# Norms between layers of a four-layer kernel: the last tile's squares go from ScalarE straight to TensorE, two norms share a root, and weights are asked for ahead of a wait

## The chip, the cores and the metric

The kernel runs on one core of one Trainium2 chip. The metric is the time of one execution on the device, in microseconds (us); lower is better. The times below are medians of several executions.

## The reference

The kernel computes four residual layers on 512 tokens of width 1024, all in fp32. What matters here is what stands between the layers: each begins with an RMS norm of the residual x, and the first block ends with a norm whose output feeds the next norm.

```python
def rms_norm(x, g):
    xf = x.astype(jnp.float32)
    y = xf * lax.rsqrt(jnp.mean(xf * xf, axis=-1, keepdims=True) + EPS)
    return (y * g.astype(jnp.float32)).astype(x.dtype)

# first block: an even layer (convolution and RWKV), then an odd one (attention over selected keys)
for l in range(2):
    h = rms_norm(x, norm_g[l]) * (1.0 + scale[:, None, :]) + shift[:, None, :]
    ...
    x = x + gate[:, None, :] * out
x = rms_norm(x, final_g)
# second block: a linear recurrence (lru), then attention with a forget gate (fox)
h = rms_norm_2(x, norm_g_2[0]); x = x + lru_mixer(h, ...)
h = rms_norm_2(x, norm_g_2[1]); x = x + fox_mixer(h, ...)
return rms_norm_2(x, final_g_2)
```

## The kernel before

x lies transposed, as 8 tiles of 128 channels by 512 tokens. Every projection is done at fp32 precision by three matmuls: the weight w and the input h are each split into a rounded part (`w_hi`, `h_hi`) and the rest (`w_lo`, `h_lo`). A weight block of 128 columns comes by DMA into one of four `raw` buffers (SyncE's queue, `weights_in`, L429), ScalarE rounds it in two halves (`round_half`, L463), GpSimd makes the rest in two halves (`rest_half`, L481), and TensorE multiplies (`project`, L498 to L500; the fox values `project_values`, L539 to L541). A raw buffer may be overwritten once GpSimd has made the rest of the block four places earlier; a split buffer (two of them, NSPLIT) is free once TensorE has projected the block two places earlier.

The program of each engine is written out by hand: `merge` interleaves streams of steps by due times that stand in the code, and all waits are on semaphores. So each engine runs a fixed list in order, and a wait holds back all that stands behind it on that engine. SyncE's list of transfers is such a list too (`sync_program`, L3005 on).

Each layer ends with an output projection in 16 half blocks (cb, part), cb being one of 8 tiles of x: `out_tensor`, `out_scalar`, `out_vector`. When a tile's second part is projected, VectorE adds it to x (L991, L993). ScalarE squares each tile (`square_scalar`, L749), and VectorE adds the squares of the tiles into one buffer `squares` (`square_vector`, L759). After the last one TensorE multiplies `squares` by a column of ones, to sum over channels into PSUM (`square_tensor`, L768: 4 matmuls in the program, 8 records in the trace, as each runs in two passes). Then ScalarE takes the root (`root_scalar`, L791), VectorE the reciprocal (L837), and TensorE spreads it over the partitions by 4 matmuls with the identity (`norm_tensor`, L828). Then VectorE makes the normed tiles (L874), ScalarE `h_hi` (L806, L808), and VectorE or GpSimd `h_lo` (L888, L890), and the first projection of the next layer can begin. The first normed tile also waits for the end of the output stage on all engines (`ended`).

Ahead of the lru layer there are two norms in a row (`scaled=True`). The tiles are squared twice, once as they are and once times the gain `final_g`, and `squares` has two halves (`which` 0 and 1). TensorE sums both (8 matmuls). After the first root and reciprocal VectorE scales the second sum by it (L847, L850), ScalarE takes a second root (L796), and VectorE makes the second reciprocal (L853, L856); `spread2` is what the layer's input needs, `spread` what the residual needs.

In the fox layer GpSimd adds a causal mask to the key bias (L2991), whose rows SyncE reads back from DRAM after it has written there the running sums of the forget gate ("key sums", L3009), which VectorE makes in a chain of small operations beside the value projections. The value blocks are called v(part, b) below, part 0 or 1, b 0 to 3; behind v(1, 3) stand q0, k0, q1, k1 and so on. The layers' norms are called by the layer that they feed: odd, lru, fox, final.

## Time and profile before

| what | us |
|---|---|
| median of 3 runs | 1917.3 |
| lowest and highest | 1914.47, 1918.16 |
| the profiled execution, its own time | 1917.06 |
| its span from first to last instruction | 1915.3 |
| TensorE busy (share of the span) | 1764.4 (92%) |
| VectorE, ScalarE, GpSimd busy | 1314.2, 784.9, 803.2 |

The profiled execution's time is 1.8 us above its span. A row of the timeline reads: start and duration in us, engine (PE TensorE, DVE VectorE, ACT ScalarE, POOL GpSimd, SPq SyncE's queue), source line, operation, output and inputs, count, and in brackets the time that the engine sat idle before it and what ended that.

### The profile page before, as it was taken

To read this page: it belongs to the slowest core of one execution; us is meant where nothing else is said; L and a number is where in the kernel's file an instruction comes from. 1 tells how busy PE (TensorE), PEld (TensorE's weight loads), DVE (VectorE), ACT (ScalarE), POOL (GpSimd) and SP (SyncE) were. 2 spreads that over 40 slices of the span, in tenths; PEclk is the share of its full clock that TensorE was granted. 3 is DMA by queue.
4 is the path that set the end of the run, shared out by engine and by line. 5 is a ranking of instruction groups with operands and counts; after the bars stand their busy time and mean duration, and the time that the engine had idled before them with its cause. 6 is when DMAs were issued, how large, how long until landed. Compare 5 with 4: busy or idle time off the path is not lost.

```text
span 1915.3 us, 33665 instructions
## 1 busy us (share of the span) xinstructions
PE 1764.4 (92%) x13616; PEld 1313.6 (69%) x13616; DVE 1314.2 (69%) x2382; ACT 784.9 (41%) x1454; POOL 803.2 (42%) x719
## 2 busy tenths in 40 slices
PE   5999999999999959999889999898799898899987
PEld 5677777777776647765766666586577676677756
DVE  7689999999998756247996565524787617155553
ACT  3424324324333352355334344433477523244442
POOL 3534334334333234556862111343355554444433
PEclk9999999999999989989999999998899898999998
DMA  7312212212212123211221011021322130433312
GB/s 280 96 50 92 88 46 89 90 46 84 95 46 90 68 69 104 97 58 64 88 68 50 29 42 34 24 97 44 110 78 82 58 106 30 152 126 121 103 50 88
DMA packets 51882, 154.80 MB, mean 81 GB/s; under 512 B 5888, under 2 KB 12032, under 8 KB 51600
## 3 DMA queue, kind: packets, MB, share of 16 engines
q1 hardware_dynamic: 51728, 152.65, 23.9%
q8 instruction: 109, 1.79, 0.4%
q14 instruction: 45, 0.37, 0.1%
HBM read 150.50 MB, written 2.13 MB: 80 GB/s over the span
## 4 chain that ended last, share of the span: by engine, by line
PE 67%; DVE 22%; ACT 5%; issue 2%; DMA 1%; POOL 1%; SPq 0%; DVEq 0%; ACTq 0%; POOLq 0%
PE bank L498 16%; PE bank L500 15%; PE bank L499 15%; PE bank L1206 6%; DVE ya L1517 4%; PE bank L2171 3%; PE bank L2159 2%; PE bank L2193 2%; DVE tables L1427 1%; PE bank L2556 1%; PE bank L2796 1%; DVE score L2288 1%; DVE best L2285 1%; PE bank L2811 1%; DVE h_lo L972 1%
## 5 line engine op out<-in xcount | busy, mean ns | idle before, releaser
L481 POOL TENSOR_TENSOR w_lo<-raw,w_hi 128x512 fp32r<-128x512 f32 (+2 forms) x434 | 560.3, 1311 | 801.8 <-ACT w_hi L463 801.8
L498 PE MATMUL bank<-h_hi,w_hi 128*128 128x512 f32 x1368 | 594.5, 435 | 59.7 <-POOL h_lo L1009 27.5
L500 PE MATMUL bank<-h_hi,w_lo 128*128 128x512 f32 x1368 | 543.1, 397 | 0.0
L499 PE MATMUL bank<-h_lo,w_hi 128*128 128x512 f32 x1368 | 542.0, 396 | 0.0
L498 PEld LDWEIGHTS bank<-h_hi,w_hi 128*128 128x128 f32 x1368 | 261.9, 191 | 161.0 <-issue 94.7
L463 ACT ACTIVATE w_hi<-raw 128x512 fp32r<-128x512 f32 (+2 forms) x434 | 241.6, 600 | 305.1 <-PE bank L500 226.8
L499 PEld LDWEIGHTS bank<-h_lo,w_hi 128*128 128x128 f32 x1368 | 262.8, 192 | 59.5 <-issue 15.5
L500 PEld LDWEIGHTS bank<-h_hi,w_lo 128*128 128x128 f32 x1368 | 261.4, 191 | 58.9
L1517 DVE SCALAR_TENSOR_TENSOR ya<-padded,vecs,ya 128x512 f32<-128x512 f32 x240 | 200.1, 834 | 1.7
L2228 ACT ACTIVATE probs<-probs,small 128x512 f32<-128x512 f32 x64 | 46.3, 724 | 109.0 <-DVE small L2211 108.6
L2865 DVE CUSTOM_DVE_ANT_0 fox_probs<-bank,fox_keybias 128x128 f32<-128x128 f32 (+3 forms) x64 | 28.8, 488 | 84.5 <-PE bank L2796 84.3
L498 PE MATMUL bank<-own_hi,w_hi 128*128 128x512 f32 x208 | 82.4, 396 | 1.0 <-DVE own_lo L972 1.0
L500 PE MATMUL bank<-own_hi,w_lo 128*128 128x512 f32 x208 | 82.1, 395 | 0.0
L499 PE MATMUL bank<-own_lo,w_hi 128*128 128x512 f32 x208 | 82.0, 394 | 0.0
L2208 DVE CUSTOM_DVE_ANT_0 probs<-bank,bias 128x512 f32<-128x512 f32 x64 | 44.1, 689 | 40.9 <-PE bank L2159 40.8
L993 DVE SCALAR_TENSOR_TENSOR x<-bank,mod,x 128x512 f32<-128x512 f32 x16 | 12.0, 750 | 86.2 <-PE bank L500 86.2
L2944 ACT ACTIVATE fox_probs<-fox_probs,fox_small 128x128 f32<-128x128 f32 (+3 forms) x64 | 35.5, 555 | 78.1 <-DVE fox_small L2871 78.1
L2159 PE MATMUL bank<-keys,q 128*128 128x512 f32 x128 | 65.4, 592 | 0.0
L1206 PEld LDWEIGHTS bank<-W,W 64*64 64x64 f32 x1792 | 55.4, 135 | 14.1 <-issue 7.1
L1206 PE MATMUL bank<-W,W 64*64 64x64 f32 x1792 | 60.9, 220 | 3.7 <-DVE W L1575 2.9
L2171 PE MATMUL bank<-probs_t,values 128*128 128x512 f32 x128 | 59.9, 612 | 3.1 <-DVE small L2218 1.9
L759 DVE TENSOR_TENSOR squares<-squares,sq 128x512 f32<-128x512 f32 x42 | 39.2, 944 | 28.7 <-ACT sq L749 27.6
(392 smaller groups left out, 2906.9 us busy)
## 6 DMA issues: line engine op xcount, KB each, us to landing
raw<-even_in SPq DMA_DIRECT2D x57, 512.0 KB, 3.6
raw<-odd_in SPq DMA_DIRECT2D x39, 512.0 KB, 3.5
raw<-ada SPq DMA_DIRECT2D x32, 512.0 KB, 3.5
raw<-fox_in SPq DMA_DIRECT2D x25, 512.0 KB, 3.5
raw<-lru_in SPq DMA_DIRECT2D x24, 512.0 KB, 3.5
ada_first<-ada SPq DMA_DIRECT2D x16, 512.0 KB, 13.8
raw<-even_out SPq DMA_DIRECT2D x16, 512.0 KB, 3.5
raw<-odd_out SPq DMA_DIRECT2D x16, 512.0 KB, 3.4
```

Source lines behind the costliest of these rows:

```text
L463: e.activation(k.w_hi[s % NSPLIT][:, at], k.raw[n % NRAW][:, at], ACT.Copy).then_inc(*did("rounded", key, half))
L481: e.tensor_tensor(k.w_lo[s % NSPLIT][:, at], k.raw[n % NRAW][:, at], k.w_hi[s % NSPLIT][:, at].bitcast(F32), ALU.subtract).then_inc(*did(" ...
L498: e.matmul(out, hi[:, w], x[i][0], start=start and i == 0, stop=False, skip_group_check=True)
L499: e.matmul(out, hi[:, w], x[i][1], start=False, stop=False, skip_group_check=True)
L500: m = e.matmul(out, lo[:, w], x[i][0], start=False, stop=stop and i == kt - 1, skip_group_check=True)
L759: e.tensor_tensor(total, total, sq[nth % 2][:, :], ALU.add).then_inc(*did("made", "square", s, i, which))
L1206: return e.matmul(out, lhsT, rhs, start=start, stop=stop, skip_group_check=True)
L1517: e.scalar_tensor_tensor(y, u[:, j:j + T], w(j), y, ALU.mult, ALU.add).then_inc(*did("tapped", q, j))
L2159: e.matmul(bank[:, :], k.Q[:, head, t * P:(t + 1) * P], k.keys[:, :], start=True, stop=True, skip_group_check=True).then_inc(*did("multipl ...
L2171: m = e.matmul(bank[:, :], k.values[:, j, :], k.probs_t[head % 2][:, j, :], start=j == 0, stop=j == TT - 1, skip_group_check=True)
L2208: e.tensor_tensor_reduce(prob, logits, bias, 1.0, 3 * NEG, ALU.add, ALU.max, mx).then_inc(*did("made", "reduced_" + s, i))
L2228: e.activation(prob, prob, ACT.Exp, bias=mx, scale=scale, accum_out=total).then_inc(*did("activated", "exp_" + s, i))
```

## The change

At the end of each output projection (four places) three things change. ScalarE takes up the square root's table and squares tile 6 one half block earlier, and squares tile 7 before it rounds the next weight block, not after. VectorE adds up tiles 0 to 6 alone and does so before x of tile 7. TensorE sums `squares` (tiles 0 to 6) and then, by 4 more matmuls into the same PSUM columns, the squares of tile 7 from ScalarE's buffer.

Ahead of lru the second weighting of tile 7 is done by TensorE: its 4 matmuls have two columns on the other side, ones and `final_g` squared (made once by VectorE in `gain_squares_vector`). The second norm's root is no longer taken from the first reciprocal: with s0 and s1 the two sums, VectorE makes a = s0/D + eps and b = s1 + eps·D·a, ScalarE takes the roots of b/D and of a, and VectorE the reciprocals; the spread that the layer's input needs comes first.

SyncE asks for two more lru weight blocks ahead of the gates' weights, and for four more blocks of the fox layer, v(1, 2) to k0, ahead of the key sums; before, one of them stood behind the key sums and three behind the first reads of the key bias.

```diff
-def square_tensor(k, e, need, did, s, both=False):
+def square_tensor(k, e, need, did, s, both=False, sq=None):
     for which in range(2 if both else 1):
         for j in range(TT):
             at = which * TT + j
-            for w in need(("made", "square", s, DT - 1, which), ("pooled", "constants"), *stat_free(k, s)):
+            for w in need(("made", "square", s, DT - 1 if sq is None else DT - 2, which), ("pooled", "constants"),
+                          *stat_free(k, s)):
                 e.wait_ge(*w)
             m = e.matmul(k.stat[:, at:at + 1], k.squares[:, which, j * P:(j + 1) * P], k.ones[:, 0:1],
                          start=at == 0, stop=True, skip_group_check=True)
+    for j in range(TT if sq else 0):
+        for w in need(("activated", "square", s, DT - 1, 0), ("made", "gain_squares") if both else None):
+            e.wait_ge(*w)
+        out = k.stat[:, 0:2 * TT].rearrange("p (w j) -> p w j", w=2)[:, 0:2 if both else 1, j]
+        m = e.matmul(out, sq[0][:, j * P:(j + 1) * P], k.gain_squares[:, 0:2] if both else k.ones[:, 0:1],
+                     start=False, stop=True, skip_group_check=True)
     m.then_inc(*did("multiplied", "squares", s))
...
 def root_scalar(k, e, need, did, s, stage, scaled=False):
     old = PREVIOUS[s]
+    if scaled:
+        for w in need(("made", "scaled", s, 1)):
+            e.wait_ge(*w)
+        e.activation(k.rms[:, 2, :], k.rms[:, 2, :], ACT.Sqrt, scale=1.0 / D).then_inc(*did("activated", "root2", s))
+        e.activation(k.rms[:, 0, :], k.rms[:, 0, :], ACT.Sqrt).then_inc(*did("activated", "root", s))
+        return
...
 def norm_vector(...):
-    one, two, root = (k.rms[:, i, :] for i in range(3))
-    inverse_vector(k, e, need, did, s)
     if scaled:
-        for w in need(("made", "inverse", s), ("multiplied", "squares", s)):
+        one, two, root = (k.rms[:, i, :] for i in range(3))
+        for w in need(("multiplied", "squares", s), ("activated", "sqrt_ready", PREVIOUS[s])):
             e.wait_ge(*w)
-        e.tensor_tensor(root, k.stat[:, TT:2 * TT], one, ALU.mult).then_inc(*did("made", "scaled", s, 0))
+        e.tensor_scalar(one, k.stat[:, 0:TT], 1.0 / D, EPS, ALU.mult, ALU.add).then_inc(*did("made", "scaled", s, 0))
         for w in need(("made", "scaled", s, 0)):
             e.wait_ge(*w)
-        e.tensor_tensor(root, root, one, ALU.mult).then_inc(*did("made", "scaled", s, 1))
+        e.scalar_tensor_tensor(root, one, EPS * D, k.stat[:, TT:2 * TT], ALU.mult, ALU.add).then_inc(
+            *did("made", "scaled", s, 1))
         for w in need(("activated", "root2", s)):
             e.wait_ge(*w)
-        e.reciprocal(root, root).then_inc(*did("made", "scaled", s, 2))
-        for w in need(("made", "scaled", s, 2)):
-            e.wait_ge(*w)
-        e.tensor_tensor(two, root, one, ALU.mult).then_inc(*did("made", "inverse2", s))
+        e.reciprocal(two, root).then_inc(*did("made", "inverse2", s))
+    inverse_vector(k, e, need, did, s)
...
 def out_scalar(...):
             yield b + 0.99
+            if (cb, part) == (DT - 1, 1):
+                square_scalar(k, e, need, did, nxt, cb, [("made", "x", s, cb)], sq, both=bool(gain))
             round_ahead(k, e, need, did, k.nth[name, cb, part] + NSPLIT)
-            if part == 0:
-                continue
-            if cb == DT - 1:
+            if (cb, part) == (DT - 1, 0):
                 for w in need(("multiplied", "spread", s)):
                     e.wait_ge(*w)
                 e.activation(k.rms[:, 0, :], k.ones[:, 0:TT], ACT.Sqrt).then_inc(*did("activated", "sqrt_ready", s))
-            for i in range(max(cb - 1, 0), cb if cb < DT - 1 else DT):
-                square_scalar(k, e, need, did, nxt, i, [("made", "x", s, i), ("vecs_in",)], sq, both=bool(gain))
+            if cb and part == (cb < DT - 1):
+                square_scalar(k, e, need, did, nxt, cb - 1, [("made", "x", s, cb - 1), ("vecs_in",)], sq, both=bool(gain))
                 if gain:
-                    square_scalar(k, e, need, did, nxt, i, [], sq, 1, gain(i), True)
+                    square_scalar(k, e, need, did, nxt, cb - 1, [], sq, 1, gain(cb - 1), True)
...
 def sync_program(k, e):
-    weights_in(k, e, need, k.order["lru", 0] + NRAW)
+    weights_in(k, e, need, k.order["lru", 0] + NRAW + NSPLIT)
     load(k.gates_w[:, :, :], t["lru_gates"], "lru_gates_in", *k.ended("lru_norm"))
-    weights_in(k, e, need, k.order["fox_v", 0, 2] + NRAW)
+    weights_in(k, e, need, k.order["fox_v", 1, 2] + NRAW)
     load(k.key_sums[:, :], k.rows[:, 2, :], "key_sums_out", ("made", "fox_sums"))
-    weights_in(k, e, need, k.order["fox_v", 0, 3] + NRAW)
```

On ScalarE at the norm ahead of lru, before the change, with the names of the semaphores that a row waits for in brackets (`sq` holds one tile's squares, `w_hi` the rounded weights, `rms` the sums and roots):

```order
L463 ACTIVATE w_hi_23<-raw_19 128x512 [waits projected,raw0]
L463 ACTIVATE w_hi_23<-raw_19 128x512
L463 ACTIVATE w_hi_24<-raw_20 128x512 [waits projected,raw1]
L463 ACTIVATE w_hi_24<-raw_20 128x512
L956 ACT_TABLE_LOAD
L956 ACTIVATE rms<-ones 128x4
L749 ACTIVATE sq_126<-x 128x512 [waits made]
L749 ACTIVATE sq_127<-x,vecs 128x512 [waits made]
L749 ACTIVATE sq_126<-x 128x512 [waits made]
L749 ACTIVATE sq_127<-x,vecs 128x512 [waits made]
L791 ACTIVATE rms<-bank,few 128x4 [waits multiplied]
L796 ACTIVATE rms<-rms,few 128x4 [waits made]
```

And with the change:

```order
L465 ACTIVATE w_hi_24<-raw_20 128x512 [waits projected,raw0]
L465 ACTIVATE w_hi_24<-raw_20 128x512
L976 ACT_TABLE_LOAD
L976 ACTIVATE rms<-ones 128x4
L751 ACTIVATE sq_127<-x 128x512 [waits made]
L751 ACTIVATE sq_128<-x,vecs 128x512 [waits made]
L751 ACTIVATE sq_127<-x 128x512 [waits made]
L465 ACTIVATE w_hi_25<-raw_21 128x512 [waits projected,raw1]
L465 ACTIVATE w_hi_25<-raw_21 128x512
L812 ACTIVATE rms<-rms 128x4 [waits made]
L813 ACTIVATE rms<-rms 128x4
```

The square root's table and both squares of tile 6 now stand ahead of the rounding of the last weight block, tile 7 is squared once and ahead of it, and the two roots stand next to each other.

On VectorE at the same place, before:

```order
L993 SCALAR_TENSOR_TENSOR x<-bank,mod_9,x 128x512 [waits projected]
L759 TENSOR_TENSOR squares<-squares,sq_126 128x512 [waits made,activated]
L759 TENSOR_TENSOR squares<-squares,sq_127 128x512 [waits made,activated]
L759 TENSOR_TENSOR squares<-squares,sq_126 128x512 [waits made,activated]
L759 TENSOR_TENSOR squares<-squares,sq_127 128x512 [waits made,activated]
L837 RECIPROCAL rms<-rms 128x4 [waits activated]
L847 TENSOR_TENSOR rms<-bank,rms 128x4 [waits multiplied,made]
L850 TENSOR_TENSOR rms<-rms 128x4 [waits made]
L853 RECIPROCAL rms<-rms 128x4 [waits activated]
L856 TENSOR_TENSOR rms<-rms 128x4 [waits made]
L874 SCALAR_TENSOR_TENSOR normed_128<-x,gain_product,bank 128x512 [waits rest_made,pooled,rounded,multiplied]
```

And with the change:

```order
L761 TENSOR_TENSOR squares<-squares,sq_127 128x512 [waits made,activated]
L761 TENSOR_TENSOR squares<-squares,sq_128 128x512 [waits made,activated]
L1020 SCALAR_TENSOR_TENSOR x<-bank,mod_10,x 128x512 [waits projected]
L868 TENSOR_SCALAR rms<-bank 128x4 [waits multiplied]
L871 SCALAR_TENSOR_TENSOR rms<-rms,bank 128x4 [waits made]
L875 RECIPROCAL rms<-rms 128x4 [waits activated]
L858 RECIPROCAL rms<-rms 128x4 [waits activated]
L894 SCALAR_TENSOR_TENSOR normed_129<-x,gain_product,bank 128x512 [waits rest_made,pooled,rounded,multiplied]
```

The last x stands behind the sums of tile 6, nothing is added up behind it, and of the five small operations on `rms` four are left.

On SyncE in the fox layer, before (rows with `raw` are weight blocks; `fox_key_sums` is the write of the key sums, `fox_keybias` the read back):

```order
L437 DMA raw_20<-fox_v 128x1024 [waits rest_made]
L437 DMA raw_21<-fox_v 128x1024 [waits rest_made]
L3009 DMA fox_key_sums<-fox_probs_t_167 16x512 [waits made]
L437 DMA raw_22<-fox_v 128x1024 [waits rest_made]
L3039 DMA fox_keybias_169<-fox_key_sums 128x128 [waits key_sums_out]
L3039 DMA fox_keybias_170<-fox_key_sums 128x128
L3039 DMA fox_keybias_169<-fox_key_sums 128x256
```

And with the change:

```order
L439 DMA raw_22<-fox_v 128x1024 [waits rest_made]
L439 DMA raw_23<-fox_v 128x1024 [waits rest_made]
L439 DMA raw_20<-fox_v 128x1024 [waits rest_made]
L439 DMA raw_21<-fox_in 128x1024 [waits rest_made]
L439 DMA raw_22<-fox_in 128x1024 [waits rest_made]
L3035 DMA fox_key_sums<-fox_probs_t_168 16x512 [waits made]
L3064 DMA fox_keybias_170<-fox_key_sums 128x128 [waits key_sums_out]
L3064 DMA fox_keybias_171<-fox_key_sums 128x128
```

The write of the key sums now has v(1, 2), v(1, 3), q0 and k0 ahead of it.

## Rows read from the trace of the kernel before

**Rows 1.** The page, part 4: shares of the chain that ended last, by engine.

```profile
PE 67%; DVE 22%; ACT 5%; issue 2%; DMA 1%; POOL 1%; SPq 0%; DVEq 0%; ACTq 0%; POOLq 0%
```

**Rows 2.** The timeline at the odd norm, all engines.

```profile
810.00 0.75 DVE L993 SCALAR_TENSOR_TENSOR x<-bank,mod,x 128x512 f32<-128x512 f32 x1 [8.46 <-PE bank L500]
810.06 1.15 ACT L463 ACTIVATE w_hi<-raw 128x512 fp32r<-128x512 f32 x2 [4.45 <-PE bank L500]
810.77 2.48 POOL L481 TENSOR_TENSOR w_lo<-raw,w_hi 128x512 fp32r<-128x512 f32 x2 [3.06 <-ACT w_hi L463]
...
814.83 1.87 PE L768 MATMUL bank<-ones,squares 128*128 128x1 f32 x8 [4.86 <-DVE squares L759]
...
819.37 0.75 DVE L874 SCALAR_TENSOR_TENSOR normed<-x,gain,bank 128x512 f32<-128x512 f32 x1 [2.17 <-PE bank L828]
```

**Rows 3.** The timeline at the lru norm, all engines.

```profile
1317.90 0.75 DVE L993 SCALAR_TENSOR_TENSOR x<-bank,mod,x 128x512 f32<-128x512 f32 x1 [6.76 <-PE bank L500]
...
1323.32 3.58 PE L768 MATMUL bank<-ones,squares 128*128 128x1 f32 x16 [5.45 <-DVE squares L759]
...
1327.46 3.78 PE L828 MATMUL bank<-ident,rms 128*128 128x128 f32 x16 [0.56 <-DVE rms L837]
...
1331.28 1.41 DVE L874 SCALAR_TENSOR_TENSOR normed<-x,gain_product,bank 128x512 f32<-128x512 f32 x2 [2.74 <-PE bank L828]
```

**Rows 4.** The timeline at the fox norm, all engines.

```profile
1579.26 0.69 DVE L991 TENSOR_TENSOR x<-bank,x 128x512 f32<-128x512 f32 x1 [6.08 <-PE bank L500]
...
1583.56 1.05 PE L768 MATMUL bank<-ones,squares 128*128 128x1 f32 x8 [4.33 <-DVE squares L759]
...
1587.29 1.41 DVE L874 SCALAR_TENSOR_TENSOR normed<-x,vecs,bank 128x512 f32<-128x512 f32 x2 [2.17 <-PE bank L828]
```

**Rows 5.** The timeline at the final norm, all engines.

```profile
1902.19 0.63 ACT L749 ACTIVATE sq<-x 128x512 f32<-128x512 f32 x1 [2.82 <-DVE x L991]
...
1903.60 1.05 PE L768 MATMUL bank<-ones,squares 128*128 128x1 f32 x8 [2.18 <-DVE squares L759]
...
1905.22 1.98 PE L828 MATMUL bank<-ident,rms 128*128 128x128 f32 x8 [0.57 <-DVE rms L837]
```

**Rows 6.** Windows: busy time of PE, PEld, DVE, ACT, POOL, granted clock, DMA share.

```profile
813.00:815.00 2.00, 0.17 (x1) 0.18 (x2) 1.39 (x2) 0.77 (x2) 0.25 (x1) 0.52 0.33 66
```

**Rows 7.** The timeline of SyncE's queue in the fox layer.

```profile
1627.06 0.34 SPq L3009 DMA_DIRECT2D fox_key_sums<-fox_probs_t  x1
1627.45 0.42 SPq L437 DMA_DIRECT2D raw<-fox_v  x1
...
1632.73 1.25 SPq L437 DMA_DIRECT2D raw<-fox_v  x1
```

**Rows 8.** The timeline of TensorE in the fox layer's value blocks.

```profile
1632.99 0.50 PE L539 MATMUL bank<-w_hi,h_hi 128*128 128x512 f32 x1 [1.54 <-POOL w_lo L481]
...
1638.35 0.39 PE L541 MATMUL bank<-w_hi,h_lo 128*128 128x512 f32 x1
1643.65 0.79 PE L539 MATMUL bank<-w_hi,h_hi 128*128 128x512 f32 x1 [4.91 <-POOL w_lo L481]
...
1651.91 0.39 PE L498 MATMUL bank<-h_hi,w_hi 128*128 128x512 f32 x1
```

**Rows 9.** The timeline of GpSimd in the fox layer.

```profile
1622.96 3.00 POOL L481 TENSOR_TENSOR w_lo<-raw,w_hi 128x512 fp32r<-128x512 f32 x2 [4.26 <-ACT w_hi L463]
...
1656.29 1.71 POOL L2991 TENSOR_TENSOR fox_keybias<-fox_keybias,causal 128x128 f32<-128x128 f32 x4
```

**Rows 10.** The timeline of VectorE and GpSimd, at two places where both run.

```profile
835.20 2.52 POOL L481 TENSOR_TENSOR w_lo<-raw,w_hi 128x512 fp32r<-128x512 f32 x2 [21.95 <-ACT w_hi L463]
...
837.54 0.19 DVE L2262 TENSOR_SCALAR wi<-bank 128x32 f32<-128x32 f32 x1 [1.86 <-PE bank L2113]
...
1348.30 4.95 POOL L481 TENSOR_TENSOR w_lo<-raw,w_hi 128x512 fp32r<-128x512 f32 x4 [2.96 <-ACT w_hi L463]
1348.33 1.26 DVE L2496 TENSOR_TENSOR lru_aux<-lru_aux 128x12 f32<-128x12 f32 x1
```

47 lines of the change are left out of this document (28 added, 19 removed).

## The prediction

> **What bounds the kernel now.** I read the page's chain first: two thirds of the span hang on TensorE [rows 1], so an edit pays only where TensorE stands still. The view of waits then names two kinds of standstill that the change touches: at each norm TensorE waits for VectorE's `squares`, and in the fox layer it waits for `w_lo` of the value blocks. I read the timelines of all five places.
>
> At a norm the reader is to see one chain with nothing beside it. Odd: x of tile 7 from 810.00, roundings from 810.06, TensorE's sum only at 814.83, normed tile at 819.37 [rows 2]. From x to the normed tile it takes 9.37 us at odd, 13.38 at lru [rows 3], 8.03 at fox [rows 4]. The first projection follows the normed tile and runs at the pace at which VectorE and ScalarE deliver tiles, so whatever the normed tile gains reaches the end.
>
> In the fox layer TensorE stood still for 1.54 and 4.91 us before the last two value blocks, v(1, 2) and v(1, 3) [rows 8]. Their weights were asked for at 1627.45 and 1632.73, behind the key sums at 1627.06 [rows 7]. v(1, 3) ran from 1643.65 to 1651.91, 8.26 us, where v(1, 2) has 23 steps in 5.36 us, 0.233 each, so about 5.6 for the block [rows 8]: the second idle had brought the clock down.
>
> **The norms, part by part.** Removed from the chain: ScalarE's roundings, the table and tile 6's squares, VectorE's last additions. Tile 6's work moves under the last half block of the projection. At odd that is 24 matmuls of 0.233 us, 5.6 us; a rounding of 1.15 stands ahead of it, and all that lay between the rounding's end (811.21) and the sum (814.83) took 3.62 [rows 2], tile 7 included. It fits. Without that cover it would cost at most these 3.6 us. At fox the half block is shorter, but no table load stands there; at final it was early before too.
>
> The sum over tiles 0 to 6 runs right behind the projection, at full clock: 8 records in 1.05 us as at fox [rows 4], against 1.87 at odd [rows 2]. Now tile 7:
>
> Odd: x ends at 810.75, the square (0.63 [rows 5]) at 811.4, its 8 records (1.05) at 812.5. From the sum's end to the normed tile it took 2.67 (816.70 to 819.37 [rows 2]), with the spread at the half clock. That gives 815.2, a gain of **4.2**. With the spread at full clock (about 1.0 less, below) it would be 814.2; but the first normed tile also waits for GpSimd's last subtraction, which ended at 813.25 and now starts some 1.25 later, as the rounding stands behind the square: 814.5. That is what is late next. Ends 4.2 and 4.9.
>
> Lru: x ends at 1318.65, the square at 1319.3. TensorE has 16 records of tiles 0 to 6 from 1317.9, about 2.0 at full clock, to 1319.9, then 8 of tile 7 (the second column costs nothing, since a record is bound by loading its 128 columns of weights, of which there are as many) to 1320.8. Then two small VectorE operations, a root, a reciprocal: I take 1.0 with the handovers, where root and reciprocal took 0.56 (1326.90 to 1327.46 [rows 3]). Then only `spread2`, half of the 16 records that took 3.78: 1.9. Normed at 1323.8 against 1331.28, a gain of **7.5**; 8.5 with the spread at full clock. GpSimd's subtraction ends at about 1322.5, before it.
>
> Fox: x ends at 1579.95, square 1580.6, sum 1581.7; 2.68 behind it (1584.61 to 1587.29 [rows 4]) gives 1584.4, with the faster spread 1583.4, held at 1583.7 by GpSimd as at odd. Ends 2.9 and 3.6.
>
> Final: no rounding, no subtraction. The square ends at 1902.82, the sum at 1903.9 instead of 1904.65 [rows 5]: **0.75**, and up to 0.9 more from the spread, which took 1.98.
>
> The spreads are a matter of the clock. The granted clock was down to 0.52 in the stretch from 813 to 815 [rows 6], so it fell at about 813.1, while at final the sum, 2.2 us after the last matmul, still ran in 1.05, and the spread behind it in 1.98 [rows 5]. If the clock falls at the same instants as before, the new spreads at odd (from 813.1) and lru lie behind the fall, those at fox and final ahead of it. An estimate for a spread at full clock is half of 1.98, about 1.0. By the instants: 4.2 + 7.5 + 3.6 + 1.65 = **17.0**. All at the half clock: 15.4. All at full: 18.7.
>
> The Trainium skill ("TensorE: Matmul & The Clock Gate", What's actually happening) says that the throttled state is the default and that activity releases it. Taken so that the sums now filling the pause count as activity, all four spreads would run at full clock and the sum be the 18.7. No row here shows a pause filled so, and I stay at 17.0.
>
> VectorE's memset and one product for `final_g` squared stand early in the odd output stage, where it waited 6.76 us for TensorE ahead of an x [rows 3]: nothing.
>
> **The fox weights.** The raw buffer for v(1, 2) is free when GpSimd has made the rest of v(0, 2), that for k0 when it has made that of v(1, 1): 1622.96 + 3.00 = 1625.96 [rows 9]. That is ahead of the key sums' 1627.06 [rows 7], so all four requests go out in time and the key sums don't go later. Then v(1, 2) follows on v(1, 1), whose last matmul ended at 1632.99 − 1.54 = 1631.45, and v(1, 3) on it: two blocks of about 5.48 (the first matmul of v(1, 2) lasted 0.50 against 0.39 as it came out of an idle, and without that a step is (5.36 − 0.11) / 23 = 0.228) put q0 at 1642.4 instead of 1651.91 [rows 8]. Gain **9.5**. From below, the two idles alone are 6.45; from above I take 9.7, as an idle also costs a refill. The cover of the moved key-bias reads: they go out behind the key sums' write (1627.06 [rows 7]) and are needed by GpSimd's first mask, at 1656.29 before [rows 9], now about 1646.6. The two lru blocks asked for earlier gain nothing: no wait of ScalarE for an lru block stands in the view of waits.
>
> **The sum** against the profiled execution: 1917.06 − 17.0 − 9.5 = **1890.6**. It lies 0.24 under the median of 1917.3, which changes nothing. Within 0.2% (3.8 us) a measurement can't tell this kernel from no change.
>
> **Rivals.**
>
> The small operations get caught by GpSimd. Its subtraction at odd, lru and fox now runs beside VectorE's operations on `rms`. Beside GpSimd a 128x12 addition took 1.26 us [rows 10]. If the new ones waited like that, each until a half of the subtraction (1.24 [rows 2]) is over, odd and fox lose up to 1.5, lru up to 1.9: 1890.6 + 4.9 = 1895.5. Against it: a TENSOR_SCALAR from PSUM, the form of the first new one, took 0.19 at 837.54, inside a subtraction that ran from 835.20 to 837.72 [rows 10]. Chance 0.1.
>
> The Trainium skill ("SBUF — State Buffer", Who interferes with whom) says that a VectorE operation with two SBUF inputs, or in a mode that uses both port pairs, is locked out while GpSimd reads, and one with a single SBUF input is not. The addition at 1348.33 agrees. By the rule alone none of the new ones would wait, since each has one SBUF input or reads PSUM.
>
> The fox requests gain nothing, because DMA or GpSimd hold v(1, 2) and v(1, 3) anyway: 1900. Against it: GpSimd's rests come one block apart, 5.5 us, so with v(1, 1)'s at 1625.96 those of v(0, 2) and v(0, 3), which free the two buffers, come at about 1609.6 and 1615, some 17 us before they were asked for at 1627.45 and 1632.73 [rows 7, 9]. Chance 0.05.
>
> TensorE's sum of tile 7 finds ScalarE late (the table load waits for an old spread, or the rounding for its block): then the norms give half, 1899. The rounding started 0.06 after x did [rows 2], so its weights were there. Chance 0.04.
>
> Slower than before: the key-bias reads come too late. They hang on SyncE's request for k0, and that on GpSimd's rest of v(1, 1). Were that rest late by d, all reads would be; they have about 10 us before the first mask waits. GpSimd would hold up q1 and k1 behind that mask, and TensorE with them. It eats the whole gain from d = 10 + 26.5, about 37 us, where the margin at the start is 1.1 us (1625.96 against 1627.06). Nothing in that stretch lasts so long. Price at d = 45: 1917.06 + 8 = 1925. Chance 0.01.
>
> The change doesn't do what it says, as the output stages end by something else: 0.01, 1917.
>
> **How the numbers follow.** The forecast's own case, the norms between 15.4 and 18.7 and the fox weights between 9.0 and 9.7, has 0.79 and spans 1888.7 to 1892.7, with 2 us for the scatter of runs (1914.47 to 1918.16 were seen) 1886.5 to 1894.7. The range of 8 in 10 reaches to the case with the small operations caught: 1886.5 to 1896.5. Faster by over 0.2%: 0.97. Same 0.015, slower 0.015.
>
> **What would show it.** In the changed kernel's timeline TensorE's first sum follows on the last matmul with no idle worth naming, and tile 7's starts about 1.5 us after that matmul, with records at full clock (1.05 for 8). From x to the normed tile: 5.2 at odd, 5.9 at lru, 4.4 at fox. At odd and fox the normed tile may be released by `w_lo`. In the fox layer TensorE has no wait for `w_lo` of a value block, the granted clock stays 1.00 and q0 follows v(1, 3). Key sums go out right when VectorE has them. The prediction is wrong if small operations on `rms` last over 1 us, if a table load turns up ahead of a root, or if a new wait opens in the fox layer ahead of q1.

## The result and the profile after

The median is 1892.62 us (1891.37 to 1895.26, 4 runs) against 1917.73 (1914.47 to 1918.41, 4 runs): a ratio of 0.9876, 95% interval 0.9861 to 0.9892. Between the medians lie 25.1 us; the ratio is worth 23.8 (20.7 to 26.7). So the kernel is faster, by 1.2%. The forecast was 1890.6. The profiled execution took 1893.53 us, 23.5 less than the one of before.

The page's chain, answering to [rows 1], is much the same, as the gains are small against the span:

```profile
PE 68%; DVE 22%; ACT 4%; issue 2%; POOL 1%; DMA 0%; SPq 0%; DVEq 0%; ACTq 0%; POOLq 0%
```

The odd norm in the timeline of the changed kernel, all engines (start, duration, engine, line, operation, tiles, shape, count, idle time before and its releaser):

```profile
811.91 0.95 PE L772 MATMUL bank<-ones,squares 128*128 128x1 f32 x8
812.12 0.75 DVE L1020 SCALAR_TENSOR_TENSOR x<-bank,mod,x 128x512 f32<-128x512 f32 x1 [1.63 <-PE bank L502]
812.90 0.63 ACT L751 ACTIVATE sq<-x 128x512 f32<-128x512 f32 x1 [3.14 <-DVE x L1020]
813.44 1.13 ACT L465 ACTIVATE w_hi<-raw 128x512 fp32r<-128x512 f32 x2
813.58 1.05 PE L778 MATMUL bank<-ones,sq 128*128 128x1 f32 x8 [0.72 <-ACT sq L751]
814.13 2.49 POOL L483 TENSOR_TENSOR w_lo<-raw,w_hi 128x512 fp32r<-128x512 f32 x2 [4.30 <-ACT w_hi L465]
815.20 1.67 PE L849 MATMUL bank<-ident,rms 128*128 128x128 f32 x8 [0.57 <-DVE rms L858]
816.91 1.40 DVE L894 SCALAR_TENSOR_TENSOR normed<-x,gain,bank 128x512 f32<-128x512 f32 x2 [1.76 <-PE bank L849]
```

Two waits of TensorE are left, 0.72 for ScalarE's square and 0.57 for the reciprocal; before it waited 4.86 for the squares [rows 2] and 0.56 for the reciprocal. The spread took 1.67, between the 2.0 of the half clock and the 1.16 that the final norm shows below: the clock fell inside it (granted clock 0.83 in the microsecond from 815, 0.50 in the next; these windows stand under e6). From x to the normed tile it is 4.79 us, 4.58 less than before.

At lru, same view:

```profile
1316.59 1.84 PE L772 MATMUL bank<-ones,squares 128*128 128x1 f32 x16
1318.29 1.03 PE L778 MATMUL bank<-gain_squares,sq 128*128 128x2 f32 x8
1318.80 2.48 POOL L483 TENSOR_TENSOR w_lo<-raw,w_hi 128x512 fp32r<-128x512 f32 x2 [4.30 <-ACT w_hi L465]
1319.36 0.16 DVE L868 TENSOR_SCALAR rms<-bank 128x4 f32<-128x4 f32 x1 [1.82 <-PE bank L778]
1319.56 0.16 DVE L871 SCALAR_TENSOR_TENSOR rms<-rms,bank 128x4 f32<-128x4 f32 x1
1319.75 0.20 ACT L812 ACTIVATE rms<-rms 128x4 f32<-128x4 f32 x1 [0.51 <-DVE rms L871]
...
1321.79 1.41 DVE L894 SCALAR_TENSOR_TENSOR normed<-x,gain_product,bank 128x512 f32<-128x512 f32 x2 [1.53 <-PE bank L849]
```

The two small operations on `rms` lie wholly inside GpSimd's subtraction (1318.80 to 1321.28) and took 0.16 each. x started at 1316.79, so the stretch is 5.00 us, 8.38 less than [rows 3]. At fox it went from 8.03 [rows 4] to 4.69 (1569.87 to 1574.56).

The final norm, same view, x first:

```profile
1879.50 0.69 DVE L1018 TENSOR_TENSOR x<-bank,x 128x512 f32<-128x512 f32 x1 [1.37 <-PE bank L502]
...
1882.52 1.16 PE L849 MATMUL bank<-ident,rms 128*128 128x128 f32 x8 [0.57 <-DVE rms L858]
1883.72 1.41 DVE L2926 SCALAR_TENSOR_TENSOR x<-x,vecs,bank 128x512 f32<-128x512 f32 x2 [1.25 <-PE bank L849]
```

4.22 us, where it was 5.78, with the spread at full clock instead of 1.98 [rows 5]. The two ends of that stretch in the kernel before:

```profile
1901.46 0.69 DVE L991 TENSOR_TENSOR x<-bank,x 128x512 f32<-128x512 f32 x1 [2.90 <-PE bank L500]
...
1907.24 1.41 DVE L2900 SCALAR_TENSOR_TENSOR x<-x,vecs,bank 128x512 f32<-128x512 f32 x2 [2.07 <-PE bank L828]
```

In the fox layer, the timelines of SyncE's queue, TensorE and GpSimd:

```profile
1605.99 7.57 SPq L439 DMA_DIRECT2D raw<-fox_in  x2
1614.30 0.34 SPq L3035 DMA_DIRECT2D fox_key_sums<-fox_probs_t  x1
1616.86 3.66 SPq L3064 DMA_DIRECT2D fox_keybias<-fox_key_sums  x8
...
1629.20 0.39 PE L543 MATMUL bank<-w_hi,h_lo 128*128 128x512 f32 x1
1629.42 0.39 PE L500 MATMUL bank<-h_hi,w_hi 128*128 128x512 f32 x1
...
1633.80 1.71 POOL L3017 TENSOR_TENSOR fox_keybias<-fox_keybias,causal 128x128 f32<-128x128 f32 x4
```

q0's first matmul starts 0.22 us after the last of v(1, 3) does, and ahead of the value blocks TensorE has no idle, where [rows 8] had two. The masks follow at once on a subtraction that began at 1631.30, so nothing waited for the reads. From the normed tile at the fox norm to the last x it took 304.94 us, 314.17 before: 9.23 less.

These four stretches and the fox layer give 17.86 + 9.23 = 27.1 us, and the two profiled executions differ by 23.5. The other 3.6 lie outside these stretches, where the change only reorders a little at the end of the output projections: the odd norm's x began at 812.12 instead of 810.00, and from the odd norm's normed tile to the lru norm's x it took 499.88 instead of 498.53.

### The profile page after: what moved, and what is told of

It is laid out like the page before. It is cut to its first block, busy times and chain, and to the rows that moved or that the text cites. A ratio compares the mean times of both kernels' runs of the same rounds, so it can differ in the third digit from the quotient of the medians.

```text
span 1891.8 us, 33719 instructions
## 1 busy us (share of the span) xinstructions
PE 1762.8 (93%) x13648; PEld 1313.5 (69%) x13648; DVE 1312.4 (69%) x2378; ACT 783.9 (41%) x1453; POOL 805.0 (43%) x719
## 4 chain that ended last, share of the span: by engine, by line
PE 68%; DVE 22%; ACT 4%; issue 2%; POOL 1%; DMA 0%; SPq 0%; DVEq 0%; ACTq 0%; POOLq 0%
PE bank L500 16%; PE bank L502 15%; PE bank L501 15%; PE bank L1231 6%; DVE ya L1542 4%; PE bank L2196 3%; PE bank L2184 3%; PE bank L2218 2%; DVE best L2310 2%; DVE score L2313 2%; DVE tables L1452 1%; DVE h_lo L992 1%; PE bank L2822 1%; PE bank L2582 1%; PE bank L2837 1%
## 5 line engine op out<-in xcount | busy, mean ns | idle before, releaser
L761 DVE TENSOR_TENSOR squares<-squares,sq 128x512 f32<-128x512 f32 x37 | 35.0, 957 | 37.0 <-ACT sq L751 36.4
```

## The experiments

Medians of these kernels move by some 2 us from one set of runs to the next, so each is read mainly by its stretches. The table holds times of one profiled execution each: the start of x at odd, x to normed tile at the four norms (at final, to the first output tile), and the fox layer's stretch. Ratio is to the kernel before, with its 95% interval.

| kernel | median, ratio | x at odd | odd | lru | fox | final | fox layer |
|---|---|---|---|---|---|---|---|
| before | 1917.73 | 810.00 | 9.37 | 13.38 | 8.03 | 5.78 | 314.17 |
| the change | 1892.62, 0.9876 (.9861-.9892) | 812.12 | 4.79 | 5.00 | 4.69 | 4.22 | 304.94 |
| e1 requests only | 1908.02, 0.9954 (.9939-.9970) | 812.07 | 9.37 | 13.38 | 8.85 | 5.88 | 303.32 |
| e2 norms only | 1899.25, 0.9910 (.9893-.9926) | 808.32 | 5.12 | 4.70 | 4.59 | 5.18 | 312.32 |
| e3 rounding first | 1891.45, 0.9871 (.9852-.9890) | 810.76 | 4.73 | 5.17 | 5.29 | 4.22 | 304.91 |
| e4 VectorE adds tile 7 | 1895.72, 0.9896 (.9876-.9916) | 809.88 | 5.93 | 8.57 | 4.95 | 5.82 | 303.65 |
| e5 two roots | 1896.42, 0.9889 (.9870-.9909) | 812.34 | 4.93 | 7.43 | 4.58 | 5.46 | 304.53 |
| e6 filled pauses | 1893.20, 0.9871 (.9846-.9897) | 810.26 | 5.14 | 5.62 | 4.59 | 4.22 | 305.64 |
| e7 four requests more | 1900.08, 0.9898 (.9869-.9928) | 810.66 | 4.74 | 4.90 | 4.58 | 5.23 | 314.30 |
| e8 lru requests undone | 1893.70, 0.9870 (.9842-.9898) | 807.56 | 4.73 | 4.92 | 4.58 | 4.23 | 304.42 |
| e9 tile 6 late | 1908.27, 0.9954 (.9939-.9970) | 807.61 | 10.28 | 12.32 | 8.89 | 5.70 | 306.44 |
| e10 last x in halves | 1894.15, 0.9864 (.9841-.9887) | 812.43 | 4.63 | 5.22 | 4.78 | 4.66 | 305.69 |
| e11 two requests more | 1890.51, 0.9865 (.9843-.9886) | 812.57 | 5.07 | 5.54 | 5.53 | 5.20 | 304.74 |

**e1, the requests alone.** The kernel before with:

```diff
-    weights_in(k, e, need, k.order["lru", 0] + NRAW)
+    weights_in(k, e, need, k.order["lru", 0] + NRAW + NSPLIT)
...
-    weights_in(k, e, need, k.order["fox_v", 0, 2] + NRAW)
+    weights_in(k, e, need, k.order["fox_v", 1, 2] + NRAW)
...
-    weights_in(k, e, need, k.order["fox_v", 0, 3] + NRAW)
```

> The kernel before with the change's order of SyncE's requests alone (the fox weights and the two lru blocks); all norms as before. My theory, that the parts of the change don't touch each other: the two waits for w_lo at value blocks are gone, the stretch from the fox norm's first normed tile to the final x is 9.2 us shorter, as in the trace of the change, and the time is 1917.7 - 9.3 = 1908.4. Rival, that the requests are worth this only together with the shorter norms (transfers that meet earlier work otherwise): 1912 or more. A second question: in the changed kernel's profile the odd norm's x ends 2.1 us later than before, though nothing of the change stands ahead of it. If that is scatter of single executions, it lies anywhere within 2 us here; if it comes with the norm part (one more small tensor, tile 6's squares ahead of the last rounding), it is back at 810.0.

The fox layer's stretch fell to 303.32, and the ratio is 8.8 us (5.8 to 11.7): the requests are worth their gain without the norms. x at odd is at 812.07 here too, without any of the norm part, so the 2.1 us need not come from it.

**e2, the norms alone.** The changed kernel with the three lines as before.

> The changed kernel with SyncE's requests as before: the norm part alone. Theory of independent parts: 17.9 us less than before, as the four stretches from x to the normed tile measure in the changed kernel's profile, so 1899.8; the fox layer has its two waits for w_lo back. Rival, that the norm part costs something elsewhere (the 2.1 us by which x at the odd norm was later, 1.4 more in the odd layer): 1903.3, with x at odd at 812 again. If those 3.5 us are scatter, x at odd falls near 810 to 812 with no rule, and the ratio tells 1899.8.

0.9910 is 17.3 us (14.2 to 20.5). The four stretches gave 17.0 (36.56 before, 19.59 here), and the fox layer's two waits of TensorE for `w_lo` are back (1.52 and 3.84 us). x at odd came at 808.32, earlier than before. The parts are independent as far as can be told: 8.8 and 17.3 beside 23.8 for the whole, whose interval of 20.7 to 26.7 holds their sum of 26.1.

**e3, the rounding ahead of tile 7's square.**

```diff
+            round_ahead(k, e, need, did, k.nth[name, cb, part] + NSPLIT)
             if (cb, part) == (DT - 1, 1):
                 square_scalar(k, e, need, did, nxt, cb, [("made", "x", s, cb)], sq, both=bool(gain))
-            round_ahead(k, e, need, did, k.nth[name, cb, part] + NSPLIT)
```

> The changed kernel with ScalarE's rounding of the next weight block ahead of tile 7's square again, at odd, lru and fox (at the final norm nothing is rounded). Theory: the square starts when the two halves of the rounding (1.13) are done, which begin with x or a little before, so each norm is 1.1 longer, 3.3 in all, and the pause of TensorE grows by as much, so that the spreads fall wholly into the half clock: up to 0.5 more at odd, 1.2 at lru (half of 16 records is behind the fall already), 0.5 at fox. 1892.6 + 3.3 to 5.5: 1897. Rival, that GpSimd's subtraction, which comes 0.6 earlier by this, gives the time back, since VectorE's normed tile waits for it: 1892.6 to 1894.

A miss: 1897 was expected, and the kernel is no slower. I had the rounding begin with x and still charged all its 1.13 us, though the square has to wait for x anyway: at odd it began at 811.88, 1.12 behind x's start, where it is 0.78 with the change. It costs the square 0.34, not 1.1. The stretches differ from the change's by -0.06, 0.17 and 0.60. At odd the rival held: GpSimd's subtraction, released by the rounding, ended at 814.01, before the spread did at 815.45, and the normed tile came 4.73 behind x. In e8, with the square first and a spread as fast, it also came at 4.73, held by GpSimd.

**e4, tile 7 added up by VectorE.**

```diff
-    square_tensor(k, e, need, did, nxt, both, sq)
+    square_tensor(k, e, need, did, nxt, both)
```

with ScalarE's second square of tile 7 at lru, and `squares(DT - 1)` behind the last x on VectorE.

> The changed kernel with tile 7's squares added up by VectorE again, and all of TensorE's sums behind that: ScalarE still squares ahead of the rounding, the root is still joint. Theory: one addition and a handover, 0.8, at odd, fox and final; at lru a second square (0.63), an addition (0.7) and 8 records more in the pause (1.0), 2.3 in all; together 4.7 if the clock stays full as long as before. As TensorE now stands still from the last matmul on, the clock falls ahead of the spreads at odd, lru and fox: 0.4, 0.8 and 0.5 more. 1892.6 + 4.7 to 6.5: 1898. Rival, that the sum over tiles 0 to 6 right behind the projection doesn't keep the clock up (the clock falls at the same instants after the last matmul of the projection): then 4.7 alone, 1897, and the spreads as in the changed kernel in time after x, shifted.

The stretches are 1.14, 3.57, 0.26 and 1.60 longer, 6.6 in all, where 4.7 to 6.5 was expected; the median gives 3.1. So the addition costs, as the first half of the theory has it. That the clock falls ahead of the spreads held at odd (the spread took 2.08) and lru (3.38 for 16 records), and not at fox, where the sum and the spread ran at full clock (1.05 and 1.16) though TensorE had waited 2.17 us ahead of the sum. How long the clock lasts isn't set by the code alone.

**e5, the lru norm's roots one after the other.** `root_scalar`, `norm_tensor` and `norm_vector` as before the change, the rest with it.

> The changed kernel with the root of the lru norm as before: root of the first sum, its reciprocal, two products, the second root, a reciprocal, a product, and TensorE's spread of the plain norm ahead of the one that the normed tile waits for. Sums and squares are as in the changed kernel. I read it by the stretch from the lru norm's x to its first normed tile, 5.00 in the changed kernel, since the medians of these kernels differ by 2 us from one trial to another. Theory: the joint root and the order of the spreads are worth the difference behind the sum's end, 4.38 before (1326.90 to 1331.28) against 2.47 (1319.32 to 1321.79), so 6.9 us here, half of it the 8 records of the other spread, and the run is 1892.6 + 1.9 = 1894.5. Rival, that the long chain before was the clock's (the 16 records ran at half clock all through): then, with the clock falling only in the spreads, 1.0 more, 6.0 us.

7.43, 2.4 more than 5.00. The timeline at lru shows what the sum of spreads doesn't:

```profile
1319.19 2.49 POOL L483 TENSOR_TENSOR w_lo<-raw,w_hi 128x512 fp32r<-128x512 f32 x2 [4.30 <-ACT w_hi L465]
...
1320.27 0.16 DVE L867 TENSOR_TENSOR rms<-bank,rms 128x4 f32<-128x4 f32 x1
...
1320.46 1.24 DVE L870 TENSOR_TENSOR rms<-rms 128x4 f32<-128x4 f32 x1
1321.74 0.30 ACT L816 ACTIVATE rms<-rms,few 128x4 f32<-128x4 f32 x1 [1.72 <-DVE rms L870]
```

The product of two SBUF tiles took 1.24 us for 4 columns and ended with GpSimd's subtraction (1321.68); the product of PSUM and SBUF just ahead took 0.16. So the rival of the caught operations exists: the change walks past it because its two new operations have one SBUF input at most. By the Trainium skill ("SBUF — State Buffer", Who interferes with whom) that is the line between the two, and both rows agree.

**e6, work in TensorE's pauses.**

```diff
+    bank = k.bank.get((PREVIOUS[s] + "_out", DT - 2))
+    for i in range(n):
+        for w in need(("made", "x", PREVIOUS[s], DT - 2)):
+            e.wait_ge(*w)
+        e.matmul(bank[:, 0:P], k.ident[:, :], k.ident[:, :], start=False, stop=True, skip_group_check=True)
```

> The changed kernel with small fp32 matmuls (identity by identity, 128x128, results unused) on TensorE in the pauses of the norms at odd, lru, fox and final: 2 between the two sums (none at lru), 2 behind tile 7's sum (4 at lru), 8 behind the spread (6 at lru, none at final). Theory: what the norms still lose is the clock, which falls in the spread at odd, lru and fox (8 records took 1.67, 1.62, and 16 took 3.24, against 1.16 at final) and comes back only at 822.7 after odd. With the fillers the granted clock stays 1.00; the spreads give 0.5, 0.7 and 0.5 of the stretches x to normed tile, and the first tiles of the projection, which run at half clock for about 3.3 us at each of the three norms, can give up to 1.6 each if VectorE and ScalarE keep up: the stretch from the normed tile to the next final x shrinks by 0 to 1.6 each. In all 1.7 to 6, 1892.6 - 3 = 1889.6. Rival, that the granted clock doesn't answer to such work, or that the tiles are paced by VectorE and ScalarE: no gain, and each filler that isn't done when a sum or spread is released delays it by up to 0.3.

No gain. The windows at odd in this kernel (busy time and count of PE, granted clock, DMA share, GB/s):

```profile
812.00:813.00 1.00, 1.00 (x10) 1.00 0.00 0
813.00:814.00 1.00, 0.98 (x6) 0.72 0.00 0
814.00:815.00 1.00, 1.00 (x7) 0.50 0.00 0
815.00:816.00 1.00, 1.00 (x6) 0.50 0.73 78
816.00:817.00 1.00, 1.00 (x8) 0.57 0.50 172
817.00:818.00 1.00, 1.00 (x10) 1.00 0.67 274
...
819.00:822.00 3.00, 2.00 (x7) 1.00 0.00 0
```

And of the changed kernel:

```profile
815.00:816.00 1.00, 0.80 (x5) 0.83 0.00 0
816.00:817.00 1.00, 0.87 (x5) 0.50 0.00 0
...
819.00:822.00 3.00, 2.59 (x6) 0.50 0.16 63
```

The clock fell to its lower level at odd with TensorE busy 0.98 to 1.00 of each microsecond from 812 on, and the spread, 2.02, was no faster. With the fillers it was back at the upper level for the projection's first tiles, which were no faster either: TensorE was then busy 2.00 of 3 us instead of 2.59, since VectorE delivers a tile each 1.32 us. The stretch behind the odd norm took 500.19 (499.88 with the change).

At fox the fillers did hold the clock. The windows there, in this kernel and in the changed one, and this kernel's normed tile:

```profile
1569.00:1577.00 8.00, 6.91 (x53) 1.00 0.47 131
```

```profile
1569.00:1577.00 8.00, 4.38 (x29) 0.78 0.38 123
```

```profile
1573.94 1.41 DVE L911 SCALAR_TENSOR_TENSOR normed<-x,vecs,bank 128x512 f32<-128x512 f32 x2 [1.62 <-POOL w_lo L483]
```

The spread took 1.16 instead of 1.62, but the normed tile then waited for GpSimd, and came 4.59 behind x instead of 4.69; the fox layer took 305.64, not less than 304.94. In each of the other twelve profiles the clock was at its lower level for 6.8 us or more around the fox norm. So the half of the theory that the clock follows such work holds at fox and fails at odd, and the half that a higher clock pays falls at both.

**e7, four requests more ahead of the key sums.**

```diff
-    weights_in(k, e, need, k.order["fox_v", 1, 2] + NRAW)
+    weights_in(k, e, need, k.order["fox_v", 1, 2] + NRAW + 4)
```

> The changed kernel with four weight requests more (q1, k1, g0, q2) ahead of the key sums' write: the rival that ended slower, brought on. The fourth waits for GpSimd's rest of q0, which ended at 1633.84 in the changed kernel, so the key sums go out at 1633.9 instead of 1614.3 and the first reads of the key bias at 1636.5. GpSimd's masks, at 1633.80 now, wait until the reads land, some 2.5 us on: 1639. Theory of the prediction (a margin eaten up, then GpSimd and TensorE held behind the mask): GpSimd is 5.2 us late behind the masks, its rest of k0 with it, and TensorE has a new wait for w_lo, 2 to 5 us, ahead of k0 or q1; slower than the changed kernel by that, 1892.6 + 3.5 = 1896, and still faster than before. Rival, that GpSimd's idle stretches (0.7 to 3.8 us ahead of each rest) and the rests' lead on TensorE take it up: within 0.5 of the changed kernel in the stretch from the fox norm's normed tile to the final x (304.94).

The fox layer took 314.30, 9.4 us more, all that the requests had gained. SyncE's queue, GpSimd and TensorE in this kernel:

```profile
1632.63 0.43 SPq L3035 DMA_DIRECT2D fox_key_sums<-fox_probs_t  x1
1637.57 3.66 SPq L3064 DMA_DIRECT2D fox_keybias<-fox_key_sums  x8
...
1641.56 0.86 POOL L3017 TENSOR_TENSOR fox_keybias<-fox_keybias,causal 128x128 f32<-128x128 f32 x2 [9.32 <-DMA fox_keybias<-fox_key_sums]
1643.98 0.86 POOL L3017 TENSOR_TENSOR fox_keybias<-fox_keybias,causal 128x128 f32<-128x128 f32 x2 [1.56 <-DMA fox_keybias<-fox_key_sums]
...
1646.11 0.79 PE L500 MATMUL bank<-h_hi,w_hi 128*128 128x512 f32 x1 [7.26 <-POOL w_lo L483]
```

The mechanism is the one forecast, larger than the 2 to 5 us expected. The reads followed the write by 4.94 us here, not 2.56, the masks waited for them twice, and TensorE, once idle for 7.26, had its clock down to 0.69 in the ten microseconds from 1640.

**e8, the lru requests undone.**

```diff
-    weights_in(k, e, need, k.order["lru", 0] + NRAW + NSPLIT)
+    weights_in(k, e, need, k.order["lru", 0] + NRAW)
```

> The changed kernel with SyncE's requests around the lru gates' load as before (the two lru blocks not asked for ahead of it); the fox part of the requests stays. Theory: nothing, no engine waits for an lru block: the stretch from the lru norm's normed tile to the fox norm's x stays 248.08, and the run within the scatter of 1892.6. Rival: ScalarE's rounding for the third and fourth lru block comes late and TensorE waits for w_lo there: over 1 us more in that stretch.

Nothing, as expected: the stretch from the lru norm to the fox norm is 248.16 against 248.08. This profile shows the early floor of the odd norm, the spread done at 811.91 and the normed tile held:

```profile
809.57 2.49 POOL L483 TENSOR_TENSOR w_lo<-raw,w_hi 128x512 fp32r<-128x512 f32 x2 [4.30 <-ACT w_hi L465]
...
810.64 1.27 PE L849 MATMUL bank<-ident,rms 128*128 128x128 f32 x8 [0.57 <-DVE rms L858]
812.29 1.41 DVE L894 SCALAR_TENSOR_TENSOR normed<-x,gain,bank 128x512 f32<-128x512 f32 x2 [1.70 <-POOL w_lo L483]
```

**e9, tile 6 late again.** The table load, tile 6's squares and their additions stand behind the last rounding and the last x, ahead of tile 7's square:

```diff
+            round_ahead(k, e, need, did, k.nth[name, cb, part] + NSPLIT)
             if (cb, part) == (DT - 1, 1):
-                square_scalar(k, e, need, did, nxt, cb, [("made", "x", s, cb)], sq, both=bool(gain))
-            round_ahead(k, e, need, did, k.nth[name, cb, part] + NSPLIT)
-            if (cb, part) == (DT - 1, 0):
                 for w in need(("multiplied", "spread", s)):
...
-            if cb and part == (cb < DT - 1):
+            if cb and part == 1:
...
+            if (cb, part) == (DT - 1, 1):
+                square_scalar(k, e, need, did, nxt, cb, [("made", "x", s, cb)], sq, both=bool(gain))
...
-            if (cb, part) == (DT - 1, 0):
-                squares(cb - 1)
...
-            if 1 < cb < DT - 1:
+            if 1 < cb:
                 squares(cb - 1)
```

> The changed kernel with tile 6 as before: ScalarE loads the square root's table and squares tile 6 only behind the last rounding, VectorE adds that up behind the last x, and TensorE's sum of tiles 0 to 6 waits for it. Tile 7's square is the last of ScalarE's, and TensorE still sums it; the root stays joint. Theory: this cover is the largest part of what the norms gained. From x to the normed tile, against the changed kernel (4.79, 5.00, 4.69, 4.22 at odd, lru, fox and final): at odd the rounding ends 0.4 behind x, then table 1.28, 0.2, two squares 1.1; the sum of tiles 0 to 6 waits for an addition 0.75 behind tile 6's square and runs in the pause, 1.0 to 1.9, and tile 7's sum behind it, another 1.0 to 1.9: 3.5 to 5 more. At lru one square more, one addition more and 16 records for 8: 5.5 to 7.5 more. Fox has no table load behind the rounding: 1.5 to 3. Final 1 to 1.5. In all 12 to 17, nearly the whole 17.9: 1892.6 + 14 = 1906.6. Rival, that the gain came from TensorE's sum of tile 7 and the joint root: then less than 6 in all, since tile 6's squares take ScalarE only 1.8.

The four stretches are 5.49, 7.32, 4.20 and 1.48 longer, 18.5 in all, and by the medians 15.7: as much as the norm part has gained. At odd in this kernel:

```profile
808.84 1.28 ACT L974 ACT_TABLE_LOAD   x1
...
810.24 1.14 ACT L751 ACTIVATE sq<-x 128x512 f32<-128x512 f32 x2
811.64 1.86 PE L772 MATMUL bank<-ones,squares 128*128 128x1 f32 x8 [4.06 <-DVE squares L761]
813.36 1.84 PE L778 MATMUL bank<-ones,sq 128*128 128x1 f32 x8
```

TensorE's sum of tile 7 is one more sum in a pause at half clock here: at odd the stretch is 10.28, even longer than the 9.37 before the change. It pays only with tile 6 out of the way.

**e10, the last x in halves.** x and the square of tile 7 in two operations of 256 tokens each, TensorE's sum of tile 7 released by halves.

```diff
+            for h in range(2) if cb == DT - 1 else (None,):
+                at = slice(0, T) if h is None else slice(h * T // 2, (h + 1) * T // 2)
```

> The changed kernel with tile 7's x and its square each cut in two (256 tokens and 256 tokens), so that ScalarE squares the first half while VectorE makes the second, and TensorE's sum of tile 7 starts with the first half. It is meant to be better than the change. Theory: 256 columns take VectorE about 0.43 and ScalarE about 0.38 (fixed part included); the second square ends at 0.86 + 0.38 = 1.25 behind x's start where one whole took 1.41, and only half of tile 7's records (0.5 of 1.05) come behind it: 0.7 less at odd, fox and final, and 0 to 0.5 at lru, where TensorE's 16 records keep it busy until 1.7 behind x. In all 2.1 to 2.6: 1890.3, with the stretches from x's start to the normed tile 4.1, 4.8, 4.0 and 3.5. Rival, that the handovers eat it (each operation more costs 0.1 to 0.2 on either engine): 0.3 a norm, not to be told from 1892.6.

Not to be told from the change: 1894.15, ratio 0.9864. At odd tile 7's sum ended 2.03 behind x's start instead of 2.51 and the spread began 2.78 behind it instead of 3.08, so 0.3 was won; the spreads of this execution took 1.72 at odd and 2.07 at final, and the stretches are -0.16, 0.22, 0.09 and 0.44 off the change's.

**e11, two requests more.** As e7 with `NRAW + 2`.

> The changed kernel with two weight requests more (q1, k1) ahead of the key sums' write, where four cost 9.4 us in the fox layer. They wait for GpSimd's rests of v(1, 2) and v(1, 3), which end at about 1622.1 and 1627.5 on the changed kernel's scale, or one block sooner. Theory, a margin: with the write at 1622.1, the reads are issued from 1624.7 (or from 1627, as they were issued 4.9 us behind the write with four requests more) and land ahead of the first mask at 1633.8: nothing lost, the fox stretch stays 303.3 to 305. Rival, that the loss grows with each request (9.4 / 4 = 2.3 each): 309.5.

The write went out at 1625.09, 47.9 behind the fox norm's normed tile where it is 39.7 with the change, the first reads at 1628.37; the masks ran at 1636.44 right behind a subtraction, and the stretch is 304.74. So it is a margin, not a price for each request.

## Why the prediction was right, point by point

**What bounds the kernel** held: what the norms and the fox layer gained where TensorE stood still reached the end, to within the 2 us by which medians scatter (e1 and e2 apart, and together).

**The norms.** Forecast 17.0, from 15.4 to 18.7; the changed profile has 17.86 (4.58, 8.38, 3.34, 1.56 for 4.2, 7.5, 3.6, 1.65). The terms: tile 7's sum ended at 2.51 behind x's start at odd, where 812.5 - 810.00 = 2.5 was forecast. Lru was undersized by 0.9: I had TensorE's tile 7 sum end 2.9 behind x and it was 2.53, the small operations 0.90 for 1.0, and from the start of the spread to the normed tile it took 1.57 for 1.9. That tile 6's work hides under the last half block is the step that carries nearly everything (e9), priced at up to 3.6 at odd if it failed, and 5.5 measured, because the price left out that both sums then run in the pause. The joint root gave 2.4 (e5), 1.1 of it because GpSimd's subtraction caught a product in e5; in the kernel before no subtraction ran there and that product took 0.16. The square ahead of the rounding brought the square 0.3 sooner (e3), and the stretches don't show that it gave anything.

One part of the gain lies in the forecast's rows without being named. At fox in the kernel before, VectorE's two additions of squares, each of two SBUF tiles, ran beside GpSimd's subtraction:

```profile
1580.03 2.93 POOL L481 TENSOR_TENSOR w_lo<-raw,w_hi 128x512 fp32r<-128x512 f32 x2 [1.68 <-ACT w_hi L463]
1581.12 2.39 DVE L759 TENSOR_TENSOR squares<-squares,sq 128x512 f32<-128x512 f32 x2 [1.16 <-ACT sq L749]
```

At odd, where the subtraction had ended, two such additions took 1.49. So some 0.9 us of the 3.34 at fox is a collision that the new order avoids.

**The clock at the spreads.** Here a step failed without harm, and that is partly luck: "If the clock falls at the same instants as before". It doesn't. In the changed profile odd's spread (1.67) was faster than forecast and fox's (1.62) slower, and the two misses all but cancel. At odd, forecast at half clock, the spread took 1.27 in e8 and 1.67 in the change, the same code, and at final 2.08 in e7 and 1.16 in the change. Kernels with the norms of before do it too: the fox sum took 1.05 in one profile [rows 4] and 1.87 in e1's. The four stretches sum to 18.70, 19.45, 18.46 and 21.34 in the change, e7, e8 and e11, which have the same norms, and 19.59 in e2; 36.56 and 37.48 in before and e1. Means of 19.5 and 37.0 give 17.5, near the 17.0, but a choice of half or full clock for one norm, as I made it, isn't readable from one trace.

**The normed tile held by GpSimd** was right where the spread was fast: e8 shows it. In the changed profile the spread ended later than the subtraction and was the releaser.

**The fox weights.** Forecast 9.5, 9.23 in the profile. The mean of ten profiles with the requests (e7 left out) is 304.8 (303.32 to 306.44), of two without 313.2 (312.32 and 314.17), so 8.4, 1.1 less than forecast. No wait for `w_lo` at a value block, clock at 1.00 and q0 right behind v(1, 3), as said.

**The lru requests** gained nothing, as said (e8).

**The margin of the reads.** I gave 10 us before the first mask waits and then a price of 1 us for each. The write goes out 39.7 us behind the fox norm's normed tile in the change, as in the kernel before (39.8), 47.9 in e11 and 59.7 in e7. The 8.2 us of e11 cost nothing, the 19.9 of e7 cost 9.4, where 19.9 - 10 = 9.9 was the rule's. That it comes so near is partly luck. The first reads of e7 are issued 22.3 later than the change's, as they also lie further behind the write, and the first mask began 9.4 later, so the reads themselves had a margin of some 13.

**Rivals.** Small operations caught: not with these forms (0.16 each), but real for a product of two SBUF tiles (1.24 in e5). The addition of [rows 10], an SBUF pair, was the right warning, and the PSUM form there the right reason for 0.1. Fox requests worthless: no (e1). ScalarE late for tile 7: no, its square began 0.03 behind x's end at odd. Reads too late: only with four requests more.

**The sum.** By the means over all profiles the parts are 17.5 + 8.4 = 25.9, where 26.5 was forecast: one a little over, one a little under. 1917.06 - 27.1 would be 1890.0, and the profiled execution took 1893.53. The difference looks like scatter of single executions, in stretches that the change hardly touches: over the thirteen profiles x at odd began from 807.56 to 812.57, and the odd layer's stretch took from 496.82 to 500.26. With the norms of before it came at 812.07 (e1), with those of the change at 807.56 and 496.86 (e8). Windows, the changed kernel first, then e8:

```profile
30.00:60.00 30.00, 27.93 (x100) 0.94 0.42 152
```

```profile
30.00:60.00 30.00, 27.59 (x104) 1.00 0.43 153
```

In the four profiles with 0.94 in this stretch (the change, e1, e10, e11) x at odd began at 812.07 or later; of the nine with 1.00 eight had it at 810.76 or earlier, and e5 at 812.34. The means are 812.3 and 809.7, so a clock that falls once near the start goes along with some 2 to 3 us.

The odd layer's 3 us go with the clock too. Added up from windows of 0.5 us, from 50 us behind the odd norm's normed tile (past the norm's own dip) to the lru norm's x, the clock was at its lower level for 6.8 to 10.2 us in the three profiles in which the layer took 496.82 to 496.88 (e3, e4, e8). It was 10.2 to 13.7 us in the four at 498.14 to 498.61 (before, e1, e2, e9), and 17.1 to 20.5 in the six at 499.88 to 500.26. That the longer time at the lower level makes the layer longer is likely, and not tested. What makes the clock fall oftener in one kernel or execution than in another, here and near the start, stays open: with one profile of each kernel, the change can't be ruled out as a cause.

## What to carry to other kernels

Where an engine waits for a chain at the end of a stage, move ahead of the last dependent tile all that doesn't depend on it (undone alone, the early table load and the tile before took back the whole gain of the norms); the tricks on the last tile itself pay only after that. A request that stands behind a write in a queue makes all that it feeds wait. The write, moved behind the requests, has a margin of its own that can be computed from two queues: two requests more were free, four cost all that the requests had gained. When medians scatter by 2 us, compare stretches between landmarks rather than medians.

## What the runs showed of the hardware

A VectorE product of two SBUF tiles of 4 columns took 1.24 us beside GpSimd's subtraction, and one of PSUM and SBUF 0.16 in the same subtraction (e5). At the odd norm the granted clock fell to 0.50 with TensorE busy 0.98 to 1.00 of each microsecond on small fp32 matmuls and was back at 1.00 from 817 on (e6); at the fox norm the same work kept it at 1.00. The Trainium skill ("TensorE: Matmul & The Clock Gate", What's actually happening) says that activity releases the lower level. That the clock was back at 1.00 from 817 with fillers, where without them it was still 0.50 from 819 to 822, agrees, and so does fox; that it fell in the midst of them at odd does not. The same instructions met the fall at different places in different executions, so one sum of 8 records took 1.05 us or 1.87.
